# Hybrid backbone, first stage: forty modulation pieces, moved out of the query and key chunks and beside the values and gates

## The reference

```
mod_x = silu(c) @ mod_w[l] + mod_b[l]         # 6 * 1024 values per stream and layer
mod_c = silu(c_ctx) @ mod_w[l] + mod_b[l]
sh1, sc1, g1, sh2, sc2, g2 = split(mod_x, 6)
hx = rms_norm(x, g) * (1 + sc1) + sh1
q, k, v, gf, gb, bv, bg = split(hx @ w_in, ...)   # even layer
q, k = axial_rope(q), axial_rope(k)               # latent tokens only
u = bv * sigmoid(bg); y = depthwise_conv31(u)     # 512 channels, 31 taps
```

## Time and profile before

| | us |
|---|---|
| median of 3 runs | 3421.58 (3416.24 to 3423.16) |
| profiled execution, its own time | 3414.93 |
| its span | 3413.2 |
| first stage, from the span's start to the next stage's first transfer | 532.65 |
| PE busy over the whole span | 2920.2 (86%) |

### The profile page before, as it was taken

The page is one execution under the profiler, slowest core; times in us unless marked ns, Lnnn a source line. Parts: engine busy times, 40 slices in busy tenths (PEclk is TensorE's granted clock), DMA queues, the critical chain, the costliest instruction groups (busy, mean ns, idle before and its releaser), DMA issues. The chain is left out here.

```text
span 3413.2 us, 51449 instructions
## 1 busy us (share of the span) xinstructions
PE 2920.2 (86%) x19780; PEld 2312.5 (68%) x19780; DVE 2078.7 (61%) x2096; ACT 1407.2 (41%) x1713; POOL 635.9 (19%) x550
## 2 busy tenths in 40 slices
PE   5998996769279999999958997699997909999998
PEld 3765785757258888888835554588886708777776
DVE  3587714644766766666722232466664478989887
ACT  2211113432045555555513334343332207767675
POOL 1076003611011222122103546000000001111111
PEclk7999997879589999999979999899998959999999
DMA  6356715744447887788741223522202349999995
GB/s 236 130 188 212 262 61 216 248 156 150 172 170 281 307 292 276 284 305 288 257 166 32 77 69 91 158 62 78 69 21 100 129 166 359 381 366 362 360 377 193
DMA packets 160767, 691.81 MB, mean 203 GB/s; under 512 B 14384, under 2 KB 78896, under 8 KB 124944
## 3 DMA queue, kind: packets, MB, share of 16 engines
q1 hardware_dynamic: 146064, 652.54, 52.4%
q0 software_dynamic: 14592, 37.76, 4.6%
HBM read 602.07 MB, written 88.18 MB: 202 GB/s over the span
## 5 line engine op out<-in xcount | busy, mean ns | idle before, releaser
L1721 DVE TENSOR_TENSOR ex_wlo<-ring,ex_whi 128x2048 fp32r<-128x2048 f32 x384 | 877.5, 2290 | 263.7 <-ACT ex_whi L1648 260.2
L1648 ACT CAST ex_whi<-ring 128x2048 fp32r<-128x2048 f32 x384 | 727.5, 1904 | 250.3 <-PE psum L1613 250.0
L1613 PE MATMUL psum<-ex_whi,ex_xh 128*128 128x512 f32 x1024 | 411.2, 402 | 10.8 <-DVE ex_wlo L1721 10.8
L1613 PE MATMUL psum<-ex_wlo,ex_xh 128*128 128x512 f32 x1024 | 400.8, 391 | 0.0
L1613 PE MATMUL psum<-ex_whi,ex_xl 128*128 128x512 f32 x1024 | 400.4, 391 | 0.0
L1613 PEld LDWEIGHTS psum<-ex_whi,ex_xh 128*128 128x128 f32 x1024 | 193.2, 189 | 61.6 <-DVE ex_wlo L1721 15.0
L542 PE MATMUL psum<-fr_whi,fr_hh 128*128 128x512 f32 x560 | 226.6, 405 | 4.5 <-DVE fr_hl L688 4.5
L1613 PEld LDWEIGHTS psum<-ex_whi,ex_xl 128*128 128x128 f32 x1024 | 193.1, 189 | 41.7
L542 PE MATMUL psum<-fr_wlo,fr_hh 128*128 128x512 f32 x560 | 220.1, 393 | 0.0
L542 PE MATMUL psum<-fr_whi,fr_hl 128*128 128x512 f32 x560 | 220.1, 393 | 0.0
L1613 PEld LDWEIGHTS psum<-ex_wlo,ex_xh 128*128 128x128 f32 x1024 | 193.5, 189 | 37.1
(11 more groups left out here) (266 smaller groups left out, 5481.3 us busy)
## 6 DMA issues: line engine op xcount, KB each, us to landing
ring<-in_moe_w SPq DMA_DIRECT2D x192, 2048.0 KB, 9.9
fr_raw<-in_mod_w SPq DMA_DIRECT2D x40, 1024.0 KB, 5.4
ring<-rec_d SPq DMA_DIRECT2D x20, 1024.0 KB, 7.2
rec_d<-fr_work SPq DMA_DIRECT2D x72, 256.0 KB, 3.2
fr_raw<-in_ev_w_in SPq DMA_DIRECT2D x14, 1024.0 KB, 6.4
h_d<-ring SPq DMA_DIRECT2D x18, 512.0 KB, 3.0
fr_arena<-in_mod_w SPq DMA_DIRECT2D x8, 1024.0 KB, 12.0
ring<-mod_d SPq DMA_DIRECT2D x11, 512.0 KB, 5.2
```

Source lines behind the costliest of these rows:

```text
L1613: last = nc.tensor.matmul(g.psum[:, 2 + i % 2, :], x[:, 4 * b + k, :], w[n][:, k, :], start=(b == 0 and k == 0 and first == 0), stop=(b == ...
L1648: nc.scalar.copy(whi[m % RING][:, :, :], slot(i)[:, 4 * b:4 * b + 4, :]).then_inc(hi_set, 1)
L1721: nc.vector.tensor_tensor(wlo[n][:, :, :], slot(i)[:, 4 * b:4 * b + 4, :], whi[n][:, :, :].bitcast(F32), ALU.subtract).then_inc(lo_set, 1)
```

## The change

Pieces 0 to 9 stay in steps 10 to 19. Pieces 10 to 39 go to steps 40 to 69, so steps 20 to 39 have none. The group ends (a group's sum to DVE, its store and the next bias load) follow their pieces: steps 18, 46, 54, 62 and 70 instead of 18, 26, 34, 42 and 50.

```diff
-        order += [(j, "mod", NT + j) for j in range(self.MODS)]
+        order += [(j, "mod", self.mod_step(j)) for j in range(self.MODS)]
+        self.mod_at = {self.mod_step(j): j for j in range(self.MODS)}
+        self.group_at = {self.mod_step(KD * n - 1) + 1: n for n in range(1, 6)}
...
+    def mod_step(self, j):
+
+        return NT + j if j < NT else 3 * NT + j
...
-                    if s >= 2 * NT - 2 and s % 8 == 2 and s <= f.MODS + NT:
-                        n = (s - NT) // 8
+                    if s in f.group_at:
+                        n = f.group_at[s]
                         store_mod(n)
...
-                    j = s - NT
-                    if 0 <= j < f.MODS:
+                    if s in f.mod_at:
+                        j = f.mod_at[s]
                         i = f.at["mod", j]
...
-                    if s >= 2 * NT - 2 and s % 8 == 2 and s <= f.MODS + NT:
-                        modulated((s - NT) // 8)
+                    if s in f.group_at:
+                        modulated(f.group_at[s])
```

## The result

The median of six runs after the change is 3439.55 us, against 3418.8 us for six of before. The ratio is 1.0058, 95% interval 1.0044 to 1.0071: slower by 15 to 24 us. Forecast were 3441 us and +19.4.

A forecast was written before the change was run, and what follows sets the result against it. POOL and DVE, slowing one another, were taken to pace the query and key chunks, PE the later steps. +24.4 + 0.4 - 8.9 + 3.5 = +19.4 us, against 3421.58 giving 3441 us, range 3429 to 3453.

The forecast's parts named there:

- The rival by which the pieces were the pace: Query and key chunks: late loads held POOL back; 38.6 us saved, 28.3 paid, 3411 us; savings above 35 us given 0.05.
- query and key chunks: Steps 20 to 39: without pieces the two chunks save 8.9 us, between 0 and 38.6, since POOL and DVE set the pace.
- pieces of steps 50 to 68, 19 x 1.22: Steps 50 to 69, which PE fills: twenty moved pieces cost 1.22 us each with nothing hiding them, +24.4 us.
- late piece, step 59: Step 59, where weights and piece come together: it repeats the wait of step 49, +0.4 us.
- from the last product of step 69 to the next stage: Stage end: last piece, DVE's sum and two stores of modulation rows delay the next stage, +3.5 us, between +1.5 and +6.
- Their landing took 4.0 to 7.1 us: Stage end: landing time read for the two `mod_d` stores; 4.0 to 4.5 us taken because the queue is empty.
- 1.1 us after the products: Stage end: the last piece follows the last products by 1.1 us, 1.3 with issue.
- The 1.7 us to the next stage: Stage end: time added between the landing of the two stores and the next stage's first transfer, at 536.1.
- PE waited under half a microsecond: Steps 40 to 49 before the change: PE's wait under the same load traffic, used to expect little waiting in steps 50 to 69.
- The walk through the chunks: Steps 20 to 39: rotary steps followed one by one, step 30 beginning 4.6 us earlier and POOL ending at 341.3, not 344.9.
- The longer store wait: Key chunk: POOL's one wait of 4.39 us in place of 3.05 may go, -1.3 us.
- The cold PE: Query and key chunks: rival in which PE, idle without pieces, stays at the lower clock; 3456 us, chance 0.08.

The follow-up runs named there:

- experiment 1: Kernel after the change, with the convolution taps of steps 20 to 39 moved to steps 40 to 69: 3404.67 us, ratio 0.9953 to the kernel before.
- experiment 2: Kernel before the change, with the same move of the taps out of steps 20 to 39: 3403.17 us, ratio 0.9954.
- experiment 8: Kernel after the change, with only the weight slice of step 43 loaded and split at step 46: 3436.6 us, ratio 1.0044.
- experiments 3: Kernel before the change, with only the query chunk freed of pieces (pieces in steps 10 to 19 and 30 to 59): 3430.19 us, ratio 1.0040.
- 4: Kernel before the change, with only the key chunk freed of pieces (pieces in steps 10 to 29 and 40 to 59): 3427.78 us, ratio 1.0022.
- experiment 5: Kernel after the change, with SP's store of the rotated key put ahead of the wait for the next rotary table: 3433.68 us, ratio 1.0035.

## Why the prediction was right, and where only its sum was

**The mechanism held.** Forecast was that POOL beside the taps sets the pace of the two chunks, and that PE's wait for a late piece would become a wait for POOL. The rows after the change show the same 8.92 us per rotary step and the wait under POOL's name; experiments 1 and 2 show the cause, since moving the taps alone takes 35.3 us and 19.5 us off the stage. The rival by which the pieces were the pace falls with them. A saving as large as its own (38.6 us) came about only when the taps were moved as well: 44.3 us up to the transpose of step 39 in experiment 1.

**The terms.** All from the two profiles, 1.88 us taken off:

| | forecast | measured |
|---|---|---|
| query and key chunks (transpose of step 39) | -8.9 | 350.20 - 341.67: -8.5 |
| pieces of steps 50 to 68, 19 x 1.22 | +23.2 | +23.3 |
| late piece, step 59 | +0.4 | +0.4 |
| late piece, steps 43 to 45 | 0 | (387.70 - 343.55) - 40.20: +3.95 |
| from the last product of step 69 to the next stage | +4.7 | 5.59 - 5.07: +0.5 |
| step 49 | 0 | -0.1 |
| sum | +19.4 | +19.5 |

For the fourth line, 40.20 us is the same distance before the change, from 350.20 to the piece of step 45 at 390.40. That the sum came out so close is luck: two errors of about 4 us cancel.

The first is the end of the stage. The step that failed is "Their landing took 4.0 to 7.1 us": the row groups every instruction on `mod_d`, and the landings in it are those of the transfers that read the rows back; the trace has none for the stores. The two lines of those reads, asked by themselves in the trace of before:

```profile
DMA to landing us min/median/max: 4.0/5.0/5.9
...
DMA to landing us min/median/max: 5.1/6.1/7.1
```

Their extremes, 4.0 and 7.1, are exactly those of the earlier trace rows. The issues of the two stores end at 551.31 and the next stage begins at 554.05, 2.7 us later. The stage's last stores to `rec_d` stood there already: before the change the next stage began 3.6 us behind their issue (529.05 to 532.65), now 4.1 us (549.93 to 554.05), so most of the new stores' landing runs beside theirs. On top of it the last piece's 1.2 us were counted twice, once among the twenty and once in "1.1 us after the products". So 4.7 us stood where 0.5 belong. The 1.7 us to the next stage in the same sum stand in no row, and its lower bound, +1.5 for a landing in 2 us, comes to +1.2 by its own terms.

The second is "PE waited under half a microsecond", read from steps 40 to 49 before the change and carried to the same steps after it. SP's loads stand there in the same order before and after, 7 us apart, and the load of the piece of step 43 has 5.5 us until PE can use it. Before, the weight slice took 6.7 us to land and was there when the piece of step 43 was issued, and that piece landed after 5.4 us, just in time. Now the slice took 8.3 us, was still on its way for 1.2 us when the piece was issued, and the piece landed after 8.0. Why the loads land later is open. Before, the stores of a modulation group and a bias load stand between the two; but experiment 8 has 8.6 us with no weight slice ahead. The row that was carried over showed that there was no wait, and not how little kept it away. The same piece waited 1.05, 1.39 and 1.57 us in experiments 3, 4 and 5, and 2.54 in experiment 1.

**The walk through the chunks.** Rotary step 27 was to end at 257.3 and ended at 258.0; step 30 was to begin at 267.2 and began at 267.2; the key's rotary steps were to take 74.1 us and took 341.66 - 269.07 = 72.6. The longer store wait did not go: it is 5.49 us now. But the last rotary step had none.

**The cold PE** happened and cost nothing in the paced steps. The granted clock fell to 0.93 and 0.90, and the transpose of step 27 took 1.09 us in place of 0.63. The rotary pace stayed at 8.92, since a spell at 1.2 GHz fits in the 2.8 us for which PE waits anyway. With pieces beside the gates PE is not idle and the clock is 1.00. The lower clock did cost time where no wait hid it: behind the late piece of step 43, 4.0 us in all for a wait of 2.4, and in experiment 5 at step 28, 1.7 us.

**The Trainium skill's rule** on the shared interface ("GPSIMD Engine Reference", section 8, Key points) agrees with these runs: the same four POOL operations take 8.9 us beside the taps and 4.06 without them. How much the taps lose was known from the earlier trace rows.

## What to carry to other kernels

A wait that is named after a transfer may only hide another one. Follow the issuing queue: if its list stands behind an engine, ask that engine's timeline for its own pace before the transfer is moved away. Work that fills another engine's time is free only where it stands; move it into a stretch where its engine has no gap and it costs its full duration, here 1.22 us apiece for a saving of 0.4. When two engines slow one another down, separate them first: here it made the place of the pieces nearly indifferent and gave more than any order of them. And a transfer that is just in time shows no wait: before a row without one is carried to another place, compare the time to landing with the time that the load has.

## What the runs showed of the hardware that was not expected

- POOL's five pauses for a store in the key chunk, 17.2 us, gave back 7.5 us when they were removed. Beside taps its step was then 8.9 us long from rotary step 33 to 36 (experiment 5). The taps take 1.49 us with POOL idle and 2.20 beside it, so a pause of POOL is not lost time for DVE.
- A 1 MB load took 5.2 to 5.5 us with one 256 KB store beside it (from 375 to 390 us after the change). At steps 41 to 43, with up to three such stores a step and the load before still on its way, it took 7.4 to 8.3 us after the change and 8.0 to 8.8 in experiment 8.
- The two small stores of modulation rows (4 x 512 floats each) were done at most 2.7 us after the end of their issue at the stage's end, with no load beside them, while 256 KB stores at steps 40 to 42 took 5 to 9 us.
